# Hybrid encoder step on one core: stores of turned operands on ScalarE's queue, values loaded per pair of heads, sample operands spread by GpSimd

## The reference

```python
xn = rmsnorm(h, g_attn)
aq, ak, av, bq, bk, bv, cq, ck, cv, dq, dk, dv, df = split(xn @ w_in)   # 1024 x 2820
a = stick_breaking(aq, [cache_a_k, ak], [cache_a_v, av])     # 4 heads of 64
b = sliding_window(bq, [cache_b_k, bk], ..., sinks, bias)    # 4 heads, 2 KV heads, window 128
c = rmsnorm(differential(cq, ck, cv, lam, bias))             # 4 heads, two maps of 32
d = forgetting(dq, dk, dv, cumsum(log_sigmoid(df + b_f)))    # 4 heads of 64
h = h + concat(a, b, c, d) @ w_out
h = h + square(relu(rmsnorm(h, g_mlp) @ w_up)) @ w_down
h = h + sigmoid(h @ w_ple_gate) * (p @ w_ple_proj)
y = rmsnorm(h, g_final)        # returned with the new K, V and gate rows
```

## Time and profile before

| | us |
|---|---|
| median of 3 executions (2262.93 to 2274.48) | 2264.15 |
| the profiled execution, its own time | 2268.79 |
| its span in the trace | 2267.2 |
| PE busy | 1896.3 (84%) |
| DVE busy | 851.6 (38%) |
| ACT busy | 645.1 (28%) |
| POOL busy | 188.0 (8%) |
| projection, the 45 units of Q and K on PE | 69.9 to 427.5 |
| attention, first scores to the last job's sample tile | 525.6 to 1171.0 |

### The profile page before, as it was taken

One profiled execution on the slowest core, in us unless ns is written; L12 is line 12 of the kernel. 1 busy time (PEld: TensorE's weight loads), 2 busy tenths in 40 slices (PEclk: granted clock), 3 DMA queues, 4 the chain that ended last, 5 costly groups with the idle time before them and its releaser, 6 DMA issues. The chain is left out here.

```text
span 2267.2 us, 28303 instructions
## 1 busy us (share of the span) xinstructions
PE 1896.3 (84%) x10134; PEld 1710.8 (75%) x10134; DVE 851.6 (38%) x1619; ACT 645.1 (28%) x1387; POOL 188.0 (8%) x272
## 2 busy tenths in 40 slices
PE   6857766775848877668779999999999999999898
PEld 6857666654747776657668889899989989998686
DVE  5211222125525636535543543333333333333334
ACT  5211111014423435423332322122212212221226
POOL 0233233300000100000101000000000000000000
PEclk9978888796667776757769999999999999999999
DMA  5555565515353443544425111111211111120202
GB/s 185 143 121 135 138 149 131 105 62 126 93 130 83 127 108 88 124 116 106 109 63 176 61 56 38 38 38 38 66 47 38 38 38 38 38 65 28 76 18 98
DMA packets 257174, 196.88 MB, mean 87 GB/s; under 512 B 178044, under 2 KB 210624, under 8 KB 257016
## 3 DMA queue, kind: packets, MB, share of 16 engines
q1 hardware_dynamic: 178312, 132.75, 21.2%
q0 software_dynamic: 60032, 57.53, 10.5%
q10 hardware_dynamic: 18688, 4.72, 0.9%
HBM read 144.29 MB, written 54.81 MB: 88 GB/s over the span
## 5 line engine op out<-in xcount | busy, mean ns | idle before, releaser
L1346 PE MATMUL outs<-v_rows,probs_turned 128*128 128x64 f32 x984 | 166.1, 325 | 112.2 <-DVE head_out L1208 84.1
L111 PE MATMUL up<-xt_hi,w_hi_even 128*128 128x384 f32 x768 | 258.0, 336 | 1.8 <-PEq L1399 1.8
L113 PE MATMUL up<-xt_hi,w_lo_even 128*128 128x384 f32 x768 | 257.8, 336 | 0.0
L112 PE MATMUL up<-xt_lo,w_hi_even 128*128 128x384 f32 x768 | 257.6, 335 | 0.0
L1346 PEld LDWEIGHTS outs<-v_rows,probs_turned 128*128 128x128 f32 x984 | 159.0, 244 | 124.8 <-DVE head_out L1208 62.1
L113 PE MATMUL down<-w_hi_odd_b,hidden_lo 128*128 128x512 f32 x576 | 224.5, 390 | 0.0
L112 PE MATMUL down<-w_lo_odd_b,hidden_hi 128*128 128x512 f32 x576 | 224.5, 390 | 0.0
L111 PE MATMUL down<-w_hi_odd_b,hidden_hi 128*128 128x512 f32 x576 | 224.0, 389 | 0.0
L1606 DVE TENSOR_TENSOR h_rows<-down,h_rows 128x1024 f32<-128x1024 f32 x72 | 88.2, 1225 | 236.4 <-PE down L113 236.4
L1571 ACT ACTIVATE hidden_rows<-up 128x384 f32<-128x384 f32 x96 | 47.3, 492 | 417.1 <-PE up L113 417.1
L1314 PE MATMUL scores<-k_turned,q_turned_straight 128*128 128x512 f32 (+5 forms) x224 | 89.9, 519 | 69.5 <-ACT probs L1038 31.1
(11 more groups left out here) (271 smaller groups left out, 3712.5 us busy)
## 6 DMA issues: line engine op xcount, KB each, us to landing
w_raw<-w_up SPq DMA_DIRECT2D x64, 256.0 KB, 2.9
w_raw<-w_down SPq DMA_DIRECT2D x64, 256.0 KB, 3.1
w_raw<-w_in SPq DMA_DIRECT2D x24, 256.0 KB, 7.6
v_rows<-value_rows SPq DMA_DIRECT2D x16, 288.0 KB, 3.7
head_rows<-head_out ACTq DMA_DIRECT2D x16, 288.0 KB, 6.4
head_rows_in<-head_rows POOLq DMA_DIRECT2D x9, 512.0 KB, 4.7
x_rows<-x_prompt SPq DMA_DIRECT2D x8, 512.0 KB, 3.7
k_cache_turned_A<-k_cache_parts POOLq DMA_DIRECT2D x16, 256.0 KB, 12.6
```

The costliest lines, as they stand in the source:

```text
L111: nc.tensor.matmul(out, xh, wh, start=first, stop=False)
L112: nc.tensor.matmul(out, xh, wl, start=False, stop=False)
L113: return nc.tensor.matmul(out, xl, wh, start=False, stop=last)
L1346: last = nc.tensor.matmul(dst, w[:, y * P:(y + 1) * P], vr[:, e, first_block(i) + y, :], start=y == 0, stop=y == nb - 1)
```

## The change

Three things, all in the projection and attention blocks.

1. The stores of turned Q and K and of turned cache keys (`qk_out`, `cache_out`) are issued by ACT, whose queue makes its descriptors in hardware, and no longer by POOL. ACT issues those of unit m-1 ahead of its work on unit m. The shapes and places are as before. POOL keeps the values and the output rows of K.
2. A job's loads lose the transfers of 64-byte runs. The main loads of Q and K take all 1152 columns, sample included, and POOL spreads the sample's part within SBUF (`spread_operands`, three copies a job); PE waits for these ahead of a sample tile's scores.
3. Values are loaded once for a pair of heads, 128 columns wide (B 64, as its heads share them), with semaphores of their own (`v_in0`, `v_in1`), for which PE waits at a pair's first value product.

The order of jobs stays A, A, B, B, C, C, D, D; the indices are rewritten so that they no longer depend on it, and one wait of A's softplus is added that this order never reaches.

```diff
-                    def qk_out(m):
-                        _, g, kind, pair, _, n = QK[m]
-                        pool.wait_ge(qk_lo, m + 1)
...
-                            nc.gpsimd.dma_start(parts(dst, g, part), src.bitcast(F32)).then_inc(st_q[m % 2], 16)
...
+                    def cache_out(x):
+                        _, u = TURN_LIST[x]
+                        if u[0] == "c":
+                            g, y = CACHE_LOADS[u[1]]
+                            act.wait_ge(c_read, x + 1)
+                            dst = kc2[g][2 * P * u[2]:2 * P * u[2] + 2 * P, 512 * y:512 * y + 512]
+                            n = caches_before(x) % CR
+                            for part in range(2):
+                                act.dma_start(parts(dst, g, part), chl[:, n, part, :].bitcast(F32)).then_inc(st_c[n], 16)
+
+                    def qk_out(m):
+                        _, g, kind, pair, _, n = QK[m]
+                        act.wait_ge(qk_lo, m + 1)
+                        dst = (k2 if kind == "k" else q2)[g][2 * P * pair:2 * P * pair + 2 * P, GT * n:GT * n + GT]
+                        for part, src in enumerate((stage_hi(m), stage_lo(m))):
+                            act.dma_start(parts(dst, g, part), src.bitcast(F32)).then_inc(st_q[m % 2], 16)
                     x = 0
                     for m, (blk, g, kind, pair, col, n) in enumerate(QK):
+                        if m:
+                            qk_out(m - 1)
+                            for y in range(x - len(TURNS[m - 1]), x):
+                                cache_out(y)
...
-                            sp.dma_start(ks[:, e, :, n:n + DEC_S].bitcast(F32), by_sequence(keys_[:, SEQ:SEQ + P])).then_inc(done, 16)
-                            sp.dma_start(spread(0, e), by_sequence(own[:, SEQ:SEQ + P])).then_inc(done, 16)
...
-                                sp.dma_start(spread(1, e)[to], by_sequence(src[:, SEQ:SEQ + P])).then_inc(done, 16)
-                            sp.dma_start(vr[:, e, :, :], vrows[:, bass.ds(V_COL[g] + HD * kvh, HD)].rearrange("(t p) d -> p t d", p=P)).then_inc(done, 16)
...
+                            if e == 0:
+                                v, nb = GROUPS.index(g) % 2, DEC_B * cached(g)
+                                w = HD if g == "B" else P
...
+                                sp.dma_start(vr[:, v, :, 0:w], vrows[:, bass.ds(V_COL[g] + w * j, w)].rearrange("(t p) d -> p t d", p=P)).then_inc(q[f"v_in{v}"], 16)
...
+                    def spread_operands(job):
+
+                        e, n = job % 2, P * cached(JOBS[job][0])
+                        job_loaded(pool, job)
...
+                        for part in range(2):
+                            nc.gpsimd.tensor_copy(by_sequence(qz[part][:, e, :])[:, :, 0:DEC_S],
+                                                  by_sequence(qt[part][:, e, SEQ:SEQ + P])).then_inc(q["spread"], 1)
+                        nc.gpsimd.tensor_copy(ks[:, e, :, n:n + DEC_S], by_sequence(kt[:, e, SEQ:SEQ + P])).then_inc(q["spread"], 1)
...
                         for job in range(len(JOBS)):
+                            spread_operands(job)
                             spread_new(job)
...
+                        if is_sample(i):
+                            pe.wait_ge(q["spread"], at("spread", 3 * (job + 1)))
```

More of the change, by code:

```diff
@@ L726, in encoder @@
             primed_sem = sem("att_primed")
-            pe_passed = sem("pe_passed_a_wait")
+            pe_passed, pool_passed = sem("pe_passed_a_wait"), sem("pool_passed_a_wait")
             NAMES = {
                 "job_in0": "loads of the even head", "job_in1": "loads of the odd head",
-                "turned": "PE: a bank of transposes is full",
+                "turned": "PE: a bank of transposes is full", "v_in0": "loads of the values of a pair of heads of A or C",
+                "v_in1": "the same of B or D", "spread": "GpSimd: the sample's queries and new keys are spread",
                 "read0": "bank 0 is evacuated", "read1": "bank 1", "read2": "bank 2",
@@ L807, in loads, with job_of, of_bias @@
             def loads(g):
-                turned = 13 if g == "C" else 9
-                return turned + {"A": 2, "B": 12, "C": 12, "D": 4 + DEC_B}[g]
-            per = {"job_in0": 16 * sum(map(loads, GROUPS)), "turned": len(ORDER), "s_full": len(UNITS),
+                return (7 if g == "C" else 5) + {"A": 0, "B": 10, "C": 10, "D": 2 + DEC_B}[g]
+            def job_of(g, e):
+                return JOBS.index((g, e))
+            def of_bias(job):
+                return sum(g in "BC" for g, _ in JOBS[:job])
+            per = {"job_in0": 16 * sum(loads(g) for g, _ in JOBS[0::2]), "v_in0": 64, "v_in1": 64, "spread": 3 * len(JOBS), "turned": len(ORDER), "s_full": len(UNITS),
                    "b_max": 2 * TILES, "m_ready": len(UNITS) - 2 * TILES, "e_ready": len(UNITS) - 2 * TILES,
@@ L816, in encoder @@
                    "stored0": 16 * 4, "stored1": 16 * 4}
-            per["job_in1"] = per["job_in0"]
+            per["job_in1"] = 16 * sum(loads(g) for g, _ in JOBS[1::2])
             per.update({f"read{x}": len(range(x, len(ORDER), 3)) for x in range(3)})
@@ L899, in body @@
                             h = 2 * j + e
+                            x = job % 2
                             kvh = j if g == "B" else h
[L901 to L904 removed]
+                            done = q[f"job_in{x}"]
                             half = HALF[g]
@@ L907, in body @@
                             keys_ = k2[g][bass.ds(P * kvh, P), :]
-                            crossed = [(slice(x, x + half), slice(y, y + half)) for z in range(0, P, 2 * half) for x, y in ((z, z + half), (z + half, z))]
-                            def by_sequence(ap):
-                                return ap.rearrange("p (b n) -> p b n", b=DEC_B)
-                            def spread(part, e):
-                                return by_sequence(qz[part][:, e, :].bitcast(F32))[:, :, 0:DEC_S]
@@ L1013, in softplus @@
                         act.wait_ge(q["s_full"], at("s_full", UNIT[(i, 0)] + 1))
+                        if i >= 2 and group(i - 2) != "A":
+                            wait_weights_free(act, i)
                         nc.scalar.activation(b, z, ACT.Abs).then_inc(q["a_abs"], 1)
@@ L1336, in values @@
                     def values(i):
-                        e, nb, c = odd(i), blocks(i), cached(group(i))
+                        e, nb, c = value_buf(i), blocks(i), cached(group(i))
+                        own = slice(0, HD) if group(i) == "B" else slice(HD * JOBS[i // TILES][1], HD * JOBS[i // TILES][1] + HD)
                         w = pt[i % 2]
@@ L1343, in values @@
                         pe.wait_ge(q["o_read"], at("o_read", i))
+                        if i % TILES == 0 and JOBS[i // TILES][1] == 0:
+                            pe.wait_ge(q[f"v_in{e}"], at(f"v_in{e}", 64 if group(i) in "CD" else 32))
                         if not is_sample(i):
                             for y in range(nb):
-                                last = nc.tensor.matmul(dst, w[:, y * P:(y + 1) * P], vr[:, e, first_block(i) + y, :], start=y == 0, stop=y == nb - 1)
+                                last = nc.tensor.matmul(dst, w[:, y * P:(y + 1) * P], vr[:, e, first_block(i) + y, own], start=y == 0, stop=y == nb - 1)
                             last.then_inc(q["o_full"], 1)
```

127 lines of the change are left out of this document (59 added, 68 removed).

## The result

| | before | changed |
|---|---|---|
| median of 4 runs each | 2264.9 us | 2440.3 us |
| lowest to highest | 2262.9 to 2274.5 | 2430.6 to 2455.5 |
| ratio to before | | 1.0771, 95% interval 1.0707 to 1.0835 |
| span of the profiled execution | 2267.2 us | 2440.8 us |
| mean granted clock of TensorE | 0.867 | 0.849 |

The change makes the kernel 7.7% slower. The forecast was 2432 us in 2340 to 2545.

A forecast was written before the change was run, and what follows sets the result against it. Q and K units were taken as bound by slow stores on few DMA engines, attention by waits for loads. 2268.8 + 225 - 57 = 2437 us, with the median 4.6 us under the profiled execution: 2432 us, range 2340 to 2545.

The forecast's parts named there:

- Part 1: Q and K stage: stores issued from ACT's queue use few engines and stand in one line, costing +225 us.
- the terms by group: Q and K stage: store time of 188 us each for A and D, 97 for B, 94 for C; 567 us.
- (a): Q and K stage: the line runs dry near 3 us in each of six pairs of units, 18 us in all.
- (b): Q and K stage: loads of weights and cached keys take engine time from the line, 20 us of 39 counted.
- Part 2: Attention loads without 64-byte runs: six DVE waits shorten by 50 us, first scores come 8 to 9 us earlier, -59 us.
- Part 3: Attention: POOL's 48 copies at 0.45 us each make PE wait 2 us together, bounds 0 and 12.
- -57: Attention: the forecast effect of Part 2 and Part 3 together in us, bounds -35 and -80.
- The signs: Expected new profile: stage 550 to 600 us, share about 0.2 or less, C quicker, DVE waits about 35 us, lower clock.
- The rival of spread stores: Q and K stage: ACT's stores spread over engines, stage 224 us, -134 us, median 2073 us; chance 0.18.

The follow-up runs named there:

- e2: The kernel before with only the new stores on ScalarE's queue and the old attention: 2491.7 us, ratio 1.0984.
- e6: The changed kernel with the low parts of the Q and K units stored from SyncE's hardware queue, between its loads: 2451.5 us.
- e3: The changed kernel, still on ScalarE's queue, with each store reshaped to one block of rows of both parts: 2077.2 us.
- e7: e4 with the loads of B's, C's and D's values issued behind the other loads of the job before: 2048.7 us.
- e11: e7 run again, unchanged, beside a repeat of e4: 2046.0 us, ratio 0.8984.
- e9: e4 with each job's small loads (bias, gates, head scalar) ahead of its large ones, with a semaphore of their own: 2045.3 us.
- e8: e7 with GpSimd also spreading a job's operands one job earlier: 2059.0 us, ratio 0.9085.
- e1: The kernel before with the new attention and the stores left in GpSimd's old program: 2218.0 us, ratio 0.9765.
- e5: The changed kernel with each store cut in two by columns, twice the issues: 2479.2 us, ratio 1.0945.
- e4: e1 with the stores reshaped to one block of rows of both parts, on GpSimd's queue: 2052.5 us, ratio 0.9041.

## Why the prediction was right

**Part 1, the line of stores.** Right in mechanism; right in size by two errors that cancel. Forecast: ACT's last unit passes at 664 us; it starts at 662.62.

```profile
662.62 0.49 ACT L444 ACTIVATE x_rows<-mm 128x384 fp32r<-128x384 f32 x1 [7.34 <-DMA q_turned_D<-x_rows]
```

Forecast +225 us; the first load of attention is issued 225.1 us later, and e2 gives +223.7. Two engines for A, B and D and four for C are seen in the shares of 0.13 and 0.26; that they are always the same is shown by a share that stays there with several stores in the queue, and by e6; that the shape alone is the cause, by e3. Against the terms by group, 188, 97, 94 and 188 us, stand 193, 105, 113 and 190 us.

The rate of 23.7 GB/s per engine was 4% low. At the 49 to 50 GB/s that two engines show, the stores' bytes take 537 to 548 us and not 567. The line runs from 76 to 683 us, where the share falls to 0.00, so 59 to 70 of its 607 us stand around the stores, and not the 38 of terms (a) and (b). Windows in which the share falls below the line's own, term (a) with 6 us in each of A, C and D, are 22 of the 594 from 76 to 670 us: 4 in A, none in B, 12 in C, 6 in D. The rest, some 37 to 48 us, would fall to the loads, term (b) with 20; that is a difference and was not measured by itself.

The prediction took its rate from a value store. Its second row, of the stores themselves, has 65 GB/s at a share of 0.33, which is 12.3 GB/s per engine. At that rate the line would take 1090 us. On ScalarE's queue an engine moves 24.5 GB/s with the same shape; why it was half of that on GpSimd's queue no run shows.

**The form of the wait was wrong.** I costed 142 issues at 0.38 us from the earlier trace rows, hidden, and forecast that ACT's longest waits would be for landings. The 142 issues take 394 us and not 54, up to 8.0 us for one of A's. Of ACT's idle time in the stage 282 us stand as "issue", up to 26.4 at a time, and 248 as waits for landings, up to 13.7. It didn't change the sum: the line of stores is as long whichever way ACT waits for it. In a kernel where the issuing engine has other work, the held issues would delay that; no run here shows such a case. In e3, where the queue drains, an issue still costs 0.6 to 0.9 us (0.45 in C), not 0.38.

**Part 2.** The forecast of -59 us is off in its largest term. The six waits fell by 30.1 us and not 50: B's first by 5.7 and 7.8 of the forecast 10.2, C's by 3.3 and 0.4 of 6, D's by 5.6 and 7.4 of 9. The step that failed is that SyncE's issue time comes off a wait in full. The last load is small but lands behind the 3 MB ahead of it, and in C the values of a pair, 1.6 MB, now stand ahead of it as well; e7 and e11, which take them out of the way, shorten C's waits to 7.0 to 9.8 us, and e9, which puts the small loads first, shortens all six to 3.2 at most. The first scores came 6.1 us sooner, not 8 to 9.

**Part 3.** A copy takes 0.30 us, not 0.45, and yet PE waits 6.5 us and not 2. The timeline of GpSimd at one of the two places, and PE's scores there:

```profile
999.21 1.15 POOL L1008 TENSOR_TENSOR head_out<-head_out,stats 128x576 f32<-128x576 f32 x1 [10.08 <-ACT stats L1069]
1000.44 1.40 POOL L1010 TENSOR_TENSOR head_out<-head_out,diff_gain_rows 128x576 f32<-128x576 f32 x1
1001.78 0.29 POOL L997 CAST q_sample_spread_straight<-q_turned_straight 128x128 fp32r<-128x128 f32 x1
```

```profile
1002.67 0.39 PE L1330 MATMUL scores<-k_sample_turned,q_sample_spread_straight 128*128 128x272 f32 x1 [3.22 <-POOL k_sample_turned L999]
```

The place was right, the norm of C; the price is not the copies' but that they stand behind that norm, which waits 10.1 us for ScalarE. I had read one place of the trace, where the norm is early. e8 moves the copies ahead of it, and the wait is gone.

**Why -57 still came out near the -50 of e1.** The waits for loads and for the copies make -30.1 + 6.5 = -23.6 us; PE's idle time in attention fell by 28.2, and with the first scores' 6.1 that is 34 us. The rest of the profile's -51.9 is PE's busy time, -17.6 us at a clock of 0.73 instead of 0.70, which I had not forecast. e2, with the old attention, shows 473.8 us of busy time, so 12 of the 17.6 us are no more than one execution of the same program differs from another. That parts 2 and 3 came near their sum owes as much to this as to the forecast.

**The signs.** Stage of 550 to 600 us: 575.8. Share of about 0.2: 0.21 in A and D, 0.24 in all. C quicker: 113 against 190. Clock lower: 0.71 from 0.82. ACT's longest waits for landings of stores: no, they are booked as issues. Six waits at 35 us: 54.9. The rival of spread stores (2073 us) did not happen with this shape, but its time was a good estimate of what spread stores give: e3 measured 2077.

## What to carry to other kernels

Before moving a transfer to a hardware queue, look at the slowest dimension of its destination: with 2 there, the DMA share stood at 0.13 and the stores stood in a line, and the same bytes as blocks of 64 rows with both parts in one transfer made the kernel 363 us faster. The software queue had hidden this, as its stores overlapped (a share of 0.57 in the stage); with the blocks it was the better of the two, as an issue of 0.6 us delays nothing on GpSimd here and stands ahead of the copies on ScalarE. A small transfer at the end of a queue is as late as all that stands ahead, and shortening one wait is worth only the distance to the next: count what is late next, and read idle time apart from PE's busy time, since the second differs by 5 to 12 us from one execution to another. One profiled execution is not the median one: compare its granted clock with those of the others.

## What the runs showed of the hardware beyond the expectation

- A full hardware queue holds the issuing engine: issues of 0.52 us at the least took up to 7.6 us (k_turned_A), and one of k_cache_turned_D 10.6 us, in the changed kernel, and 2.05 us in the median for half the bytes in e5.
- With stores of two engines on SyncE's and ScalarE's queues at once, the total stays at 0.13 and 49 to 52 GB/s.
- PE's granted clock was 1.00 (2.4 GHz) while PE worked up to 243.3 us in the changed kernel, and still in the microsecond from 244, with PE idle; it was 0.59 in the one from 245 and 0.50 (1.2 GHz) from 246 on; PE worked again from 249.6 us, and the clock was back at 1.00 from 256. In e4, with no such pause, it is 1.00 over the whole stage.
- One program of attention took 485.8 and 473.8 us of PE's busy time in two executions (before and e2), with idle times of 179.7 and 179.1; another took 458.9 to 468.1 us in seven, with 148.6 to 154.1.
